# Eight split-weight slots instead of six in an expert layer, and a closing norm taken from PSUM

## The reference

```python
logits = (t @ w_router).astype(jnp.float32)
top_vals, top_idx = lax.top_k(logits, TOP_K)
top_w = jax.nn.softmax(top_vals, axis=-1)
gates = jnp.sum(jax.nn.one_hot(top_idx, N_EXPERTS, dtype=jnp.float32) * top_w[..., None], axis=1)
out = jnp.zeros_like(t)
for e in range(N_EXPERTS):
    out = out + gates[:, e:e + 1].astype(t.dtype) * swiglu(t, w_gate[e], w_up[e], w_down[e])
...
    h = h + f
return rmsnorm(h, norm_final)
```

## Time and profile before

| | before |
|---|---|
| median of three executions | 1205.95 us |
| the profiled execution: its time, its span | 1204.75 us, 1203.0 us |
| busy share of the span | PE 96%, weight loads 80%, DVE 73%, ACT 63% |
| bytes read from HBM, mean rate | 292.90 MB, 244 GB/s |
| mean granted TensorE clock | 0.993 of full speed |
| expert steps, first gate granule to last down granule | from 710.77 us to 1186.72 us of the span |
| from there to the end | 16.3 us |

### The profile page before, as it was taken

How to read it: one execution, slowest core, us unless ns; L and a number is a source line. 1 busy time by engine, 2 the same in 40 slices (tenths; PEclk the granted TensorE clock), 3 DMA queues, 4 the chain that set the end, 5 groups by cost and what they waited for, 6 DMA issues and landing times.

```text
span 1203.0 us, 15865 instructions
## 1 busy us (share of the span) xinstructions
PE 1155.7 (96%) x5656; PEld 966.0 (80%) x5656; DVE 879.3 (73%) x989; ACT 755.6 (63%) x905; POOL 20.1 (2%) x60
## 2 busy tenths in 40 slices
PE   8999999999999999999999999999999999999994
PEld 7787788888888888887788889878887888788863
DVE  5567667665455455586666788988998899889994
ACT  6456556454444435555666457887778777877881
POOL 3000000000000001000000000000000000000000
PEclk9999999999999999999999999999999999999997
DMA  9645423668655445537225639999999999999990
GB/s 325 235 147 180 161 86 99 204 219 276 190 193 174 147 137 181 187 117 227 94 74 181 227 125 350 381 389 388 365 373 360 383 374 370 367 382 371 359 369 38
DMA packets 120266, 294.97 MB, mean 245 GB/s; under 512 B 8974, under 2 KB 33644, under 8 KB 119676
## 3 DMA queue, kind: packets, MB, share of 16 engines
q1 hardware_dynamic: 119088, 288.66, 68.1%
q0 software_dynamic: 960, 5.28, 1.2%
q10 hardware_dynamic: 140, 0.04, 0.0%
HBM read 292.90 MB, written 1.05 MB: 244 GB/s over the span
## 4 chain that ended last, share of the span: by engine, by line
PE 76%; DVE 10%; ACT 7%; issue 5%; DMA 1%; SPq 0%; POOL 0%; DVEq 0%; ACTq 0%; POOLq 0%
PE bank L1476 21%; PE bank L1478 20%; PE bank L1477 20%; DVE w_lo L1271 5%; PE bank L1854 3%; ACT w_hi L811 3%; PE bank L1855 3%; PE bank L1514 2%; ACT w_hi L628 1%; PE bank L1837 1%; DMA raw<-in_w_in 1%; PE bank L1677 1%; PE bank L1657 1%; ACT p_buf L756 1%; DVE mixed L1177 1%
## 5 line engine op out<-in xcount | busy, mean ns | idle before, releaser
L1271 DVE TENSOR_TENSOR w_lo<-raw,w_hi 128x1792 fp32r<-128x1792 f32 (+3 forms) x198 | 383.5, 1965 | 45.4 <-ACT w_hi L811 44.1
L811 ACT ACTIVATE w_hi<-raw 128x1792 fp32r<-128x1792 f32 (+3 forms) x198 | 325.9, 1659 | 100.1 <-PE bank L1478 73.6
L980 DVE TENSOR_TENSOR w_lo<-raw,w_hi 128x1536 fp32r<-128x1536 f32 (+3 forms) x144 | 242.9, 1693 | 178.7 <-ACT w_hi L628 178.1
L628 ACT ACTIVATE w_hi<-raw 128x1536 fp32r<-128x1536 f32 (+4 forms) x144 | 205.6, 1433 | 159.7 <-PE bank L1478 159.1
L1476 PE MATMUL bank<-w_hi,aT_hi 128*128 128x512 f32 (+1 forms) x592 | 235.9, 399 | 2.5 <-DVE w_lo L980 2.4
L1478 PE MATMUL bank<-w_hi,aT_lo 128*128 128x512 f32 (+1 forms) x592 | 230.4, 389 | 0.0
L1477 PE MATMUL bank<-w_lo,aT_hi 128*128 128x512 f32 (+1 forms) x592 | 230.2, 389 | 0.0
L1476 PEld LDWEIGHTS bank<-w_hi,aT_hi 128*128 128x128 f32 x592 | 111.7, 189 | 24.7 <-issue 3.6
L1478 PEld LDWEIGHTS bank<-w_hi,aT_lo 128*128 128x128 f32 x592 | 111.5, 188 | 22.8
L1477 PEld LDWEIGHTS bank<-w_lo,aT_hi 128*128 128x128 f32 x592 | 111.8, 189 | 20.3
L1854 PE MATMUL bank<-w_hi,xT 128*128 128x448 f32 x256 | 96.5, 377 | 4.8 <-DVE w_lo L1271 4.4
(11 more groups left out here) (271 smaller groups left out, 1546.2 us busy)
## 6 DMA issues: line engine op xcount, KB each, us to landing
raw<-in_moe_w_gate SPq DMA_DIRECT2D x128, 448.0 KB, 5.8
raw<-in_moe_w_up SPq DMA_DIRECT2D x128, 448.0 KB, 5.6
raw<-in_moe_w_down SPq DMA_DIRECT2D x112, 512.0 KB, 5.9
raw<-in_w_in SPq DMA_DIRECT2D x40, 768.0 KB, 4.4
raw<-in_dense_w_gate SPq DMA_DIRECT2D x22, 512.0 KB, 4.0
raw<-in_dense_w_up SPq DMA_DIRECT2D x22, 512.0 KB, 4.8
raw<-in_dense_w_down SPq DMA_DIRECT2D x11, 1024.0 KB, 4.9
raw<-in_w_in SPq DMA_DIRECT2D x20, 512.0 KB, 4.9
```

What stands on the lines that cost most here:

```text
L628: act.activation(w_hi[:, weight_slot(b, j), 0:n], raw[:, b % 2, j, 0:n], ACT.Copy).then_inc(hi_made[j], 1)
L811: act.activation(split_of(hi_slot, m), raw_of(i, n), ACT.Copy).then_inc(e_hi_made, 1)
L980: dve.tensor_tensor(w_lo[:, s, 0:n], raw[:, b % 2, j, 0:n], w_hi[:, s, 0:n].bitcast(F32), ALU.subtract).then_inc(lo_made[j], 1)
L1271: dve.tensor_tensor(split_of(lo_slot, m), raw_of(i, n), split_of(hi_slot, m).bitcast(F32), ALU.subtract).then_inc(e_lo_made, 1)
```

## The change

It does five things.

- **Eight split slots.** `W_SLOTS` is 8; slots 6 and 7 (`w_hi_more`, `w_lo_more`) lie where the second token buffer was. ACT's split of granule i now waits for PE's use of granule i - 8, and each engine splits two granules further ahead in its loop. One more split (`expert_hi(6)`, `expert_lo(6)`) stands ahead of the loop. The 12 raw slots stay.
- **One token buffer.** `xT` is one buffer of four 128-wide columns of tokens: hi and lo of the large expert once, and the small expert's 128 columns twice, by parity of the pair. Copying a quarter of the hi tokens takes ACT two instructions instead of one (16 more in all).
- **Step 15's hidden values earlier.** The small hidden values alternate between two buffers, DVE makes those of step 15 at granule (15, 18) ahead of the split there, and they are transposed after (15, 20).
- **The residual in PSUM.** In turn 16, after each of the first four down granules, PE starts bank 4 + q with a product of the identity and a quarter of `h` (both plain float32) and adds the large expert's part. After the last granule only the small expert's part is left, in the order q = 0, 2, 1, 3, and each half waits only for its own half of `y_lo`.
- **The norm from PSUM.** ACT squares the four banks with a running sum (four instructions of 128x512), DVE adds the partial sums and the epsilon, POOL takes the power, DVE scales the four banks straight from PSUM, and four transfers of 256 KB store the result. The last four `add_output`, `square_tile(4)` and `scale_tokens` go.

```diff
-RAW_SLOTS, W_SLOTS, SLOT_W = 12, 6, 1024
+RAW_SLOTS, W_SLOTS, SLOT_W = 12, 8, 1024
...
-BETWEEN = {(STEPS - 1, 22): ("hidden", STEPS - 1, 0)}
+BETWEEN = {(STEPS - 1, 20): ("hidden", STEPS - 1, 0)}
...
-        aT_hi, aT_lo, xT0, fold = regions(
+        aT_hi, aT_lo, xT = regions(
             [("aT_hi", [P, KC, S], F32R), ("aT_lo", [P, KC, S], F32R)],
-            [("xT0", [P, KC, 3 * P], F32R), ("fold", [P, HALF], F32R)])
+            [("xT", [P, KC, 4 * P], F32R)])
...
-        bT_hi, bT_lo, xT1 = regions(
+        bT_hi, bT_lo, w_hi_more, w_lo_more = regions(
             [("bT_hi", [P, KC, S], F32R), ("bT_lo", [P, KC, S], F32R)],
-            [("xT1", [P, KC, 3 * P], F32R)])
-        p_buf, pT = place("p_buf", [P, 3 * P]), place("pT", [P, 3 * P])
+            [("w_hi_more", [P, 2, SLOT_W], F32R), ("w_lo_more", [P, 2, SLOT_W], F32R)])
         qkT, s_buf = mixed[:, 0, NB:2 * NB], mixed[:, 1, NB:NB + 3 * P]
-        xT, y_of = (xT0, xT1), ((y_hi, y_lo), (y1_hi, y1_lo))
-        hT_small = [b[:, :].rearrange("p (c x s) -> p c x s", x=2, s=SMALL) for b in (hT_hi_buf,)][0]
+        hi_slot, lo_slot = (
+            [(b[:, :, :].rearrange("p j (u n) -> p (j u) n", n=SLOT_W), n) for n in (2, 3, 4, 5, 0, 1)] + [(more, 0), (more, 1)]
+            for b, more in ((w_hi, w_hi_more), (w_lo, w_lo_more)))
+        y_of = ((y_hi, y_lo), (y1_hi, y1_lo))
+        hT_small = [b[:, :].rearrange("p (c x s) -> p c x s", x=2, s=SMALL) for b in (hT_hi_buf, hT_lo_buf)]
         rope_t = mixed[:, 0, :].rearrange("p (n h d) -> p n h d", n=4, h=HEADS)
...
+        BACK_ORDER = (0, 2, 1, 3)
...
+            of, at_slot = slots[i % W_SLOTS]
+            return of[:, at_slot:at_slot + n, 0:granule_width(GRANULES[i][2])]
...
+        def small_hi(p):
+
+            return slice(P + 2 * P * (p % 2), P + 2 * P * (p % 2) + SMALL)
+
+        def small_lo(p):
+            return slice(P + 2 * P * (p % 2) + SMALL, 2 * P + 2 * P * (p % 2))
+
+        def small_both(p):
+            return slice(P + 2 * P * (p % 2), 2 * P + 2 * P * (p % 2))
 
...
-            for t in range(NT):
-                sp.wait_ge(xs_made, t + 1)
-                sp.dma_start(out[0, t * P:(t + 1) * P, :], xs[:, t, :]).then_inc(stored, 16)
-            sp.wait_ge(stored, 16 * NT)
+            for q in range(4):
+                t, part = q // 2, slice(q % 2 * NB, (q % 2 + 1) * NB)
+                sp.wait_ge(xs_made, q + 1)
+                sp.dma_start(out[0, t * P:(t + 1) * P, part], xs[:, t, part]).then_inc(stored, 16)
...
-            norm_root(4)
+            pool.wait_ge(var_made, 1)
+            pool.tensor_tensor(rstd[4], var, minus_half[:, 0:2], ALU.pow).then_inc(rstd_made, 1)
...
-                        act.wait_ge(used[i // 2], MIX[1] + BLK_MIX + 2)
+                        act.wait_ge(used[min(i // 2, 2)], MIX[1] + BLK_MIX + 2)
...
+            expert_hi(6)
...
-                act.activation(xT[p % 2][:, 2 * q:2 * q + 2, 0:P + SMALL], tokens_of(b), ACT.Copy).then_inc(x_hi_in, 1)
+                dst = xT[:, 2 * q:2 * q + 2, :]
+                act.activation(dst[:, :, small_hi(p)], tokens_of(b)[:, :, P:P + SMALL], ACT.Copy)
+                act.activation(dst[:, :, 0:P], tokens_of(b)[:, :, 0:P], ACT.Copy).then_inc(x_hi_in, 1)
...
-            second_round(act, experts, lambda: act.wait_ge(h_new, 4 + 8 * PAIRS_E))
-            square_tile(4)
+            second_round(act, experts, lambda: act.wait_ge(back_made, 8 * PAIRS_E))
+            for i, n in enumerate(BACK_ORDER):
+                act.wait_ge(back_made, 4 * (PAIRS_E - 1) + i + 1)
+                act.activation(hg[:, n // 2, n % 2 * NB:(n % 2 + 1) * NB], bank[B_BACK[n]][:, :], ACT.Square, accum_out=part_sq[:, n // 2, n % 2:n % 2 + 1]).then_inc(squared, 1)
...
+            def final_norm():
+
+                dve.wait_ge(squared, 4)
+                link(dve.tensor_tensor(var, part_sq[:, :, 0], part_sq[:, :, 1], ALU.add))
+                dve.tensor_scalar(var, var, 1.0 / D, EPS, ALU.mult, ALU.add).then_inc(var_made, 1)
+                dve.wait_ge(rstd_made, 5)
                 dve.wait_ge(gain_in, 32)
-                for t in range(NT):
-                    dve.scalar_tensor_tensor(out=xs[:, t, :], in0=h[:, t, :], scalar=rstd[N][:, t:t + 1], in1=gain[:, :],
+                for q, b in enumerate(B_BACK):
+                    t, part = q // 2, slice(q % 2 * NB, (q % 2 + 1) * NB)
+                    dve.scalar_tensor_tensor(out=xs[:, t, part], in0=bank[b][:, :], scalar=rstd[4][:, t:t + 1], in1=gain[:, part],
                                              op0=ALU.mult, op1=ALU.mult).then_inc(xs_made, 1)
 
...
+                    expert_lo(6)
...
+                    if (k, n) == (STEPS - 1, GU_N + 2):
+                        expert_hidden(r, k, SMALL)
                     if i % 2 and i + W_SLOTS < PER_ROUND * (r + 1):
                         expert_lo(i - 1 + W_SLOTS)
-                    if k < STEPS and n == (GU_N + 3 if is_small(k) else GU_N - 1):
...
+                    if k < STEPS - 1 and n == (GU_N + 3 if is_small(k) else GU_N - 1):
-                for q, b in enumerate(B_BACK):
-                    add_output(PAIRS_E * r + PAIRS_E - 1, q, b)
-            second_round(dve, experts, lambda: dve.wait_ge(h_new, 4 + 8 * PAIRS_E))
-            square_tile(4)
-            scale_tokens(4)
+            second_round(dve, experts, lambda: dve.wait_ge(back_made, 8 * PAIRS_E))
+            final_norm()
...
-                pe.wait_ge(y_lo_made, 2 * (EXPERTS * r + 2 * p + x) + 2)
+                pe.wait_ge(y_lo_made, 2 * (EXPERTS * r + 2 * p + x) + u + 1)
                 tokens = selT[:, p % 2, x, t * P:(t + 1) * P]
                 for n, y in enumerate(y_of[x]):
-                    last = pe.matmul(bank[b][:, :], tokens, y[:, u * NB:(u + 1) * NB], start=x == 0 and n == 0, stop=x == 1 and n == 1)
+                    last = pe.matmul(bank[b][:, :], tokens, y[:, u * NB:(u + 1) * NB], start=start and n == 0, stop=x == 1 and n == 1)
...
-                        last = small_product(dst, hT_hi_buf[:, part], b_hi, b_lo, start, stop)
+                        last = small_product(dst, (hT_hi_buf, hT_lo_buf)[half][:, part], b_hi, b_lo, start, stop)
...
+                        if k == STEPS and GU_N <= n < GU_N + 4:
+                            q = n - GU_N
+                            pe.wait_ge(h_new, 4 + 4 * (PAIRS_E * r + PAIRS_E - 1))
+                            pe.matmul(bank[B_BACK[q]][:, :], ident[:, :], h[:, q // 2, q % 2 * NB:(q % 2 + 1) * NB], start=True, stop=False)
...
-                for x in range(2):
-                    for q, b in enumerate(B_BACK):
-                        bring_back(r, PAIRS_E - 1, q, b, x)
+                for q in BACK_ORDER:
+                    bring_back(r, PAIRS_E - 1, q, B_BACK[q], 1, False)
```

49 lines of the change are left out of this document (27 added, 22 removed).

## The result

The changed kernel takes 1188.95 us (median of 4 runs, 1188.1 to 1190.55), the kernel before 1205.43 on the same footing (4 runs). The ratio is 0.9866 with a 95% interval of 0.9854 to 0.9879: 16.5 us faster. Predicted were 1186.0, with a range of 1179 to 1198. The profiled execution took 1188.18 us.

The account below looks back on a forecast made before the run. The prediction saw PE, DVE and ACT in a ring with too few slots. Its terms, -17.5 - 2.9 - 2.0 + 5.5 - 3.2 = -20.1, took 1204.75 to 1184.65, some 1186 us as median; range 1179 to 1198.

Parts of the forecast that it names:

- The forecast case: Whole kernel: faster, predicted 1186 us with its own range of 1181 to 1191; chance 0.62.
- term 1: Expert steps: eight split slots shorten PE's 25.2 us of waits for splits, -17.5 us.
- term 2: From the end of granule (15, 17) to turn 16's first: earlier hidden values of step 15 save time, -2.9 us.
- clock in turn 16: TensorE's granted clock no longer falls to 0.50 in turn 16, -2.0 us, between -2.0 and +2.
- term 3: Turn 16: four float32 products with `h` and the large expert's eight products are added on the path, +5.5 us.
- term 4: From the last granule to the end of the span: 13.2 us instead of 16.45, -3.2 us.
- local queues: Expert steps: the prediction said a pair at about 113 us, DVE busy 96%, is possible but not free of these.
- right: Profile signs: split waits under 8 us, pair 112 to 114 us, DVE 95% busy, no 0.50 clock before last granule.
- wrong: Profile signs: ACT waiting for `raw`, pair above 116 us, clock 0.50 under turn 16, ACT idle 2 us before squares.
- The load stream: Rival, expert pairs: loads hold only 378 GB/s, a pair takes 116.5 us, time 1194 us; chance 0.17.
- ACT held at a landing: Rival, small experts' steps: ACT reaches splits before their loads land, everything behind waits, about 1213 us; chance 0.06.
- more than I take: Rival, expert steps: no wait for splits remains and waits behind them shrink too, 1178 to 1180 us; chance 0.09.

Follow-up runs that it names:

- Six slots: The changed kernel with six split slots again instead of eight, all else of the change kept: 1203.79 us.
- slots alone: The changed kernel with step 15's hidden values late and the old end, leaving eight slots and one token buffer: 1188.32 us.
- Splits last: The changed kernel with ACT's and DVE's splits at an odd index behind all other work of that index: 1185.39 us.
- Hidden values first: The changed kernel with step 15's hidden values three granules earlier in DVE's loop, their transposed part also ahead of further splits: 1182.24 us.
- x = 0 behind: The changed kernel with the eight products of the last pair's first expert moved behind the last granule: 1187.75 us.
- both orders: The changed kernel with splits behind other work and step 15's hidden values three granules earlier in DVE's loop: 1181.08 us.
- hidden first, old end: The changed kernel with step 15's hidden values three granules earlier in DVE's loop, and the end of the kernel before: 1183.55 us.

## Why the prediction came out as it did

The forecast case came true: the kernel is faster, at 1188.95 within its own range of 1181 to 1191, and 2.95 above the predicted 1186. (The profiled execution is 3.5 above its 1184.65; the median lies 0.8 above that execution, where 1.2 was taken.) In the prediction's own terms, from the profiled executions:

| step | predicted | measured |
|---|---|---|
| term 1, to the end of (15, 17) | -17.5 | -17.5 |
| term 2, from there to (16, 16), 11.4 before | -2.9 | +0.4 |
| clock in turn 16, and term 3 | -2.0 + 5.5 | +3.5 |
| term 4, behind the last granule | -3.2 | -3.4 |
| ahead of the first gate granule | 0 | +0.4 |
| sum | -20.1 | -16.6 |

**Term 1 was right, in its size and its reason.** 438.44 us (1149.64 - 711.20) against 455.96 (1166.73 - 710.77). Its two parts came as said: counted to the first product of granule (15, 18), the last step with gate and up granules gave 2.5 us (18.10 instead of 20.61, from 1146.74 to 1167.35 before), where one split of 2.29 was taken, and the steps ahead of it 15.5, where 15.3 was. "Six slots" gives the gain back, "slots alone" has it without the rest. The reason why it is less than 25.2 was only guessed as "local queues": 23.9 us of the weight loads' waits for splits went (25.2 less 1.1 and 0.2), 5.1 came back as waits for the fold and 2.8 as waits of L1832. "Splits last" takes away the waits of L1832 and gains 3.8 us of the stretch, 3.3 of them in the three steps that had such a wait, so they, at least, did cost time.

**Term 2 is the step that failed**, and with it goes nearly all of the error, 3.3 of 3.5 us. The prediction said of DVE "ACT's split 1.9, DVE's split of that pair 2.3, still ahead of the hidden values in the queue, then 1.14", ready 5.4 us after the end of (15, 17). It took DVE to be as little behind as it had been with six slots, free by the time that ACT's split is done. In the changed kernel DVE begins one split at that point and has two more queued: 2.29 + 4.49 us (6.6 by the starts of their rows, which overlap, where the prediction had 1.9 + 2.3) ahead of the hidden values, which are ready at 1157.40, 7.8 us after. In the step before this point DVE was busy 17.53 of 18.10 us, so it had no chance to catch up. Longer lead means a longer queue, and an instruction placed by its granule comes later in time. PE's wait became 3.77 us instead of 2.1. "Hidden values first" shows the claim from the other side: in front of that queue they save 4.4 us in the stretches.

**The clock** was the second half of the same error. Turn 16 ran at the full clock, as forecast, but for its first product: 12.0 us (1161.40 to 1173.40), which is 6.5 + 5.5 and bears out term 3 with it. But the products of turn 15's last two granules, which stand between the wait and turn 16, ran at 0.56: from 1158.09, eight of them, to 1161.40 are 3.3 us, where 8 x 0.23 is 1.9. Of the 3.3 us that term 2 missed, 2.5 are the later start of the transposes (7.9 after the end of (15, 17) instead of 5.4), and 0.8 what lies behind it (3.85 instead of 3.1). That "a single wait of 2.1 us" leaves the clock alone is refuted by "six slots": a wait of 2.1 us, and the clock at 0.50.

**Term 3 was right.** A granule with a product of `h` and two of the large expert's part takes 1.33 us more (1162.54 to 1163.87), of it 0.86 for the float32 product, 5.3 in all against 5.5. "x = 0 behind" shows that its 1.9 us were on the path (1.9 in the stretch), and could have stayed in the shadow of `y_hi` and `y_lo`.

**Term 4 was right in the sum.** 13.0 us against 13.2. The squares began 3.5 us after the last granule (3.2 forecast), ended at 5.9 (6.2), and ACT's jump cost 1.0 where 0.7 was taken. DVE's wasn't quite covered: 0.5 us. The four scalings took 2.73 us instead of 2.48. Two shorter pieces made up for it: the squares, 2.4 for the four instead of 3.0, and the stores, 2.6 us behind the last scaling instead of 3.2.

The Trainium skill (Runtime: NRT & Kernel Launch, Instruction fetch mechanics) says that a taken branch out of the prefetched pages stalls the engine until the target page has been fetched. The run without the jump agrees in that a jump costs time, 1.0 us on ACT's path and 0.5 on DVE's; no run here shows the fetch itself.

**The signs.** Most of those named for "right" came: waits for splits under 8 us, DVE busy 94%, products with `h` of 0.86 us, 13.0 us behind the last granule. The pair is a little above its 112 to 114 (114.29), and DVE's waits for ACT are 26.8 us, six tenths of 43.6 and not half. Two did not come, and one named for "wrong" did: there is a slice at the low clock ahead of the last granule, in turn 15, DVE is late at its two small instructions, and ACT is idle 2.04 us ahead of its first square, 1.0 of it by its jump.

**The rivals.** The load stream did not take over: a pair ran at 388 GB/s, up to 391 with the splits last and 393 with both orders. The Trainium skill (HBM Reference, Specifications) gives about 358 GB/s as a core's share with both cores of a pair streaming and more for a lone one; these rows are above the share. ACT held at a landing did not happen in the changed kernel; in other kernels with twelve raw slots it came to at most 1.8 us, and with ten it cost 3.8. DVE as the bound for "more than I take" is not reached: 94% busy in the changed kernel, 95% with the splits last (107.54 of 113.75). The prediction's "DVE is the next bound, at 108" left out PE, which comes first: it waits for others for 2.3 of the pair's 114.29 us, so shorter waits alone can't bring a pair below about 112 (an estimate from these two numbers).

What is left open: whether the new end beats the old one beside the hidden values first (1182.24 against 1183.55 is within their ranges, and 1.0 us in the stretches).

## What to carry to other kernels

When a ring of buffers gets longer, the producers run further ahead, and what shares their queues comes later by as many splits as the lead has grown (here one double split, 7.6 us instead of 5.5): look through the queue for short work that another engine waits for, and put it ahead. A term for a wait that the change shortens should be computed with the queue of the changed kernel, not with that of the trace. And of a part that adds work on the path in order to save some behind it (here 5.3 for 3.4 us), the worth hangs on whether there is a wait that it fills.

## What the runs showed of the hardware

- The granted clock of TensorE fell to 0.50 behind a single wait of 2.1 us, and to 0.55 behind 2.08 us in which PE had been busy for 1.17 ("hidden first, old end"). It stayed at 1.00 where the wait was gone. The cost on top of the wait, in these two and in the changed kernel: eight products in 3.3 to 3.4 us instead of 1.9.
- The same program's part ahead of the experts ended between 709.1 and 712.1 us in fourteen profiled executions. Differences of 1 us between kernels could be read in the stretches from a common point on, and not in the medians: "hidden values first" is 6.7 us faster by its median and 4.4 by its stretches.
- A DMA share of 1.01 in the windows of a pair stood beside 388 and 391 GB/s, and 0.99 beside 371 before: the share rose by 2% where the rate rose by 5%.
